# A two-block transformer layer kernel on one core: sums folded in the last up block, output rows added in memory by DMA, a reordered second norm, and queries and keys projected from consecutive tokens

## The reference, cut to what matters

```python
x = x + _rmsnorm_2(mix, g_mix_post[l])
h2 = _rmsnorm_2(x, g_mlp_pre[l])
ff = jnp.einsum('bsf,fd->bsd',
                jnp.square(jax.nn.relu(jnp.einsum('bsd,df->bsf', h2, w_up[l]))), w_down[l])
x = x + _rmsnorm_2(ff, g_mlp_post[l])
```

```python
q = _partial_rope(q.reshape(b, s, N_ATT_HEADS, HEAD_DIM), positions)
k = _partial_rope(k.reshape(b, s, N_ATT_HEADS, HEAD_DIM), positions)
```

## Time and profile before

| what | us |
|---|---|
| median of 3 runs | 2628.11 |
| lowest and highest run | 2627.49 and 2632.41 |
| the profiled execution | 2632.22 |
| span of the core in it | 2630.4 |
| PE busy in the span | 2522.1 (96%) |
| DVE, ACT, POOL busy | 1557.1, 852.1, 688.8 |

### The profile page before, as it was taken

How to read it: one execution, slowest core, us unless ns; L and a number is a source line. 1 busy time by engine, 2 the same in 40 slices (tenths; PEclk the granted TensorE clock), 3 DMA queues, 4 the chain that set the end, 5 groups by cost and what they waited for, 6 DMA issues and landing times. The chain is left out here.

```text
span 2630.4 us, 31418 instructions
## 1 busy us (share of the span) xinstructions
PE 2522.1 (96%) x12016; PEld 2105.4 (80%) x12016; DVE 1557.1 (59%) x2472; ACT 852.1 (32%) x1664; POOL 688.8 (26%) x656
## 2 busy tenths in 40 slices
PE   7999999999999999989999999999989999999995
PEld 4787889987899887778888888878867788887874
DVE  5611348888778686564655612124466857768588
ACT  4212231122311132462023133330145545354452
POOL 3422223333234232322533422224210000000002
PEclk8999999999999999999999999999999999999998
DMA  7311222213231222633443122225249574766753
GB/s 249 100 49 44 67 65 60 67 43 97 81 90 49 70 95 78 217 105 124 128 144 122 41 88 65 72 78 185 90 153 274 134 201 120 195 185 165 192 120 112
DMA packets 163514, 303.45 MB, mean 115 GB/s; under 512 B 22178, under 2 KB 46498, under 8 KB 159524
## 3 DMA queue, kind: packets, MB, share of 16 engines
q1 hardware_dynamic: 144164, 255.30, 29.6%
q0 software_dynamic: 18048, 41.95, 9.0%
q10 hardware_dynamic: 1152, 4.19, 0.4%
HBM read 235.12 MB, written 57.87 MB: 111 GB/s over the span
## 5 line engine op out<-in xcount | busy, mean ns | idle before, releaser
L2236 PE MATMUL ps<-act_hi,w_hi 128*128 128x512 f32 x1344 | 541.0, 403 | 14.4 <-DVE act_lo L1503 4.1
L1053 POOL CAST w_hi<-raw 128x512 fp32r<-128x512 f32 x288 | 216.0, 750 | 1248.6 <-DMA raw<-in_w_in 797.6
L2236 PE MATMUL ps<-act_lo,w_hi 128*128 128x512 f32 x1344 | 535.9, 399 | 0.0
L2236 PE MATMUL ps<-act_hi,w_lo 128*128 128x512 f32 x1344 | 528.2, 393 | 0.0
L1624 DVE SCALAR_TENSOR_TENSOR scr<-scr,small 128x512 f32<-128x512 f32 x480 | 430.4, 897 | 15.6
L1055 POOL TENSOR_TENSOR w_lo<-raw,w_hi 128x512 fp32r<-128x512 f32 x288 | 403.9, 1403 | 23.1
L2236 PE MATMUL ps<-w_hi,act_hi 128*128 128x512 f32 (+1 forms) x960 | 384.6, 401 | 2.8 <-POOL w_lo L1055 2.1
L2236 PE MATMUL ps<-w_lo,act_hi 128*128 128x512 f32 (+1 forms) x960 | 373.7, 389 | 0.0
L2236 PE MATMUL ps<-w_hi,act_lo 128*128 128x512 f32 (+1 forms) x960 | 373.5, 389 | 0.0
L2463 PE MATMUL ps<-w_hi 128*128 128x512 f32 x896 | 350.8, 391 | 21.0 <-DVE w_lo L2015 11.3
L2463 PE MATMUL ps<-w_hi,w_lo 128*128 128x512 f32 x896 | 349.2, 390 | 0.0
(11 more groups left out here) (222 smaller groups left out, 2706.1 us busy)
## 6 DMA issues: line engine op xcount, KB each, us to landing
raw<-in_w_in SPq DMA_DIRECT2D x176, 256.0 KB, 3.3
late_hi<-h2c_d SPq DMA_DIRECT2D x21, 1024.0 KB, 8.0
vreg<-in_w_ada SPq DMA_DIRECT2D x48, 256.0 KB, 4.0
raw<-in_w_in SPq DMA_DIRECT2D x72, 128.0 KB, 2.4
x_d<-big SPq DMA_DIRECT2D x16, 512.0 KB, 4.0
late_lo<-in_w_up SPq DMA_DIRECT2D x8, 1024.0 KB, 6.5
late_lo<-in_w_up POOLq DMA_DIRECT2D x8, 1024.0 KB, 12.8
raw<-in_w_up POOLq DMA_DIRECT2D x8, 1024.0 KB, 11.4
```

Source lines behind the costliest of these rows:

```text
L1053: pool.tensor_copy(dhi, src).then_inc(w_hi_done, 1)
L2236: ins = nc.tensor.matmul(out_, lhs, rhs, start=(m == 0), stop=(m == 3 * nk - 1))
```

## The change

- **Queries and keys.** `token_block(g, B)` becomes `token_block(g if name == "v" else 0, B)`: q and k are projected from consecutive tokens in every group; v as before. ACT's copy of a turned q or k tile of groups 1 and 2 now sorts the tokens: it reads PSUM with a step of 4 or 8 elements and writes runs of 32 or 16 elements. `rotate` takes the table row of the consecutive block.
- **The second norm.** ACT's first root of B comes before `turned_copy(B - 2)`; `weight_hi(0)` moves from B = 4 to B = 2; `act_hi_of(0)` is halved over B = 5 and 6, and a half of `act_hi_of(1)` comes at B = 7. DVE makes the halves of `act_lo_of(0)` right after the `evac_out` of B = 6 and B = 7, and halves of `act_lo_of(1)` around `norm_two(7)`. SP loads the first weight quarter one block earlier.
- **POOL's order of weight adds.** In each block the add into slot 0 (`t1_sum`) is issued before that into slot 1 (`t3_sum`).
- **Sums.** In the last up block (6), at its products 0 to 4, `fold_quarter` joins the running sums of blocks 1 to 5 by five instructions of 128x2048; in block 7, `mid` is overwritten in place of added to, product 5 is added into both `sum5` and `sum3`, and three folds per tile are gone.
- **The end.** The second norm stores its rows to the output itself (`x2_d` is gone), and after `final_scale(B)` POOL issues a DMA that adds the block onto those rows in device memory. `final_scale` is spread through the last product.

```diff
-                        if B == 2:
+                        if B == 1:
                             sp.wait_ge(w_ready, NP0)
                             weight_load(0, 0)
...
-                sp.dma_start(x2_d[P * B:P * B + P, :], tokT[:, B, :]).then_inc(n_st[1], 16)
+                sp.dma_start(out[P * B:P * B + P, :], tokT[:, B, :]).then_inc(n_st[1], 16)
...
-            for B in range(NB):
-                if B >= 2:
-                    sp.wait_ge(n_y[2], B - 1)
-                sp.dma_start(res2[B % 2], x2_d[P * B:P * B + P, :]).then_inc(n_ld[2][B % 2], 16)
-                if B >= 2:
-                    sp.dma_start(out[P * (B - 2):P * (B - 1), :], tokT[:, B - 2, :]).then_inc(out_st, 16)
...
             for blk in range(BLOCKS):
+                pool.wait_ge(wc_lo, 2 * at_product(blk, 1) + 2)
+                weight_add(0, weight_quarter(blk, 0, 1), t1_sum)
                 pool.wait_ge(wq_ld[1], 16 * (blk + 1))
                 weight_add(1, weight_quarter(blk, 1, 1), t3_sum)
-                pool.wait_ge(wc_lo, 2 * at_product(blk, 1) + 2)
-                weight_add(0, weight_quarter(blk, 0, 1), t1_sum)
...
+            pool.wait_ge(n_st[1], 16 * NB)
             for B in range(NB):
                 pool.wait_ge(n_scaled, B + 1)
-                pool.wait_ge(n_ld[2][B % 2], 16 * (B // 2 + 1))
-                pool.tensor_tensor(tokT[:, B, :], tokT[:, B, :], res2[B % 2], ALU.add).then_inc(n_y[2], 1)
+                pool.dma_start(out[P * B:P * B + P, :], tokT[:, B, :], accum_op=ALU.add).then_inc(out_st, 16)
+            pool.wait_ge(out_st, 16 * NB)
...
+                    if g in (1, 2):
+                        dst = (qT if name == "qt" else kT)[:, :, :]
...
+                            dst = dst.rearrange("p k (r j) -> p k r j", r=8)[:, :, :, 16 * B:16 * B + 16]
+                            src = src.rearrange("p (k j r) -> p k r j", k=4, r=8)
+                        nc.scalar.activation(dst, src, ACT.Copy).then_inc(free_of(u), 1)
...
                 for B in range(NB):
                     if B >= 2 and r == 0:
                         turned_hi(name, B - 2)
-                    elif B >= 2:
-                        turned_copy(B - 2)
-                    if r and B == 4:
-                        weight_hi(0)
-                    if r and B == 6:
-                        act_hi_of(0)
...
                     mean_square_root(r, B, 0, n_s1[r])
+                    if B >= 2 and r:
+                        turned_copy(B - 2)
+                        if B == 2:
+                            weight_hi(0)
+                        elif B >= 5:
+                            act_hi_of((0, 0, 1)[B - 5], ((0,), (1,), (0,))[B - 5])
                     norm_second(r, B)
...
                     evac_out(r, B, 1, NB + B)
+                    if r and B >= 6:
+                        act_lo_of(0, (B - 6,))
                     if B >= 1:
                         norm_two(r, B - 1)
...
                     norm_one(r, B)
-                    if r and B == NB - 1:
-                        act_lo_of(0)
+                if r:
+                    act_lo_of(1, (0,))
                 norm_two(r, NB - 1)
...
-                    add(mid, before(6))
+                    if end:
+                        dve.wait_ge(folded, 5)
+                    add(mid, -1 if end else before(6))
...
                     add(sum5, before(5))
+                    if end:
+                        add(sum3, before(3))
                 elif p == 3:
-                    add(sum3, before(3))
-                    if end:
-                        wait_used(dve, n, t)
-                        fold(sum3, sum5, ALU.add)
+                    add(sum3, at_product(blk, 5) if end else before(3))
...
-                        fold(sum7, mid, ALU.add)
...
+            FOLDS = ((sum7, mid, ALU.add, (7, 6)), (sum3, sum5, ALU.add, (3, 5)), (sum3, mid, ALU.subtract, ()),
+                     (sum5, sum7, ALU.subtract, ()), (sum4, sum7, ALU.add, (4,)))
...
+                nc.vector.tensor_tensor(dst, dst, a, op).then_inc(folded, 1)
...
+                if blk == BLOCKS - 2 and q < 5:
+                    fold_quarter(q)
+                if n == PRODUCTS - 1:
+                    final_scale(0)
                 evict(n, 0)
+                if n == PRODUCTS - 1:
+                    final_scale(1)
                 evict(n, 1)
...
+                if n == PRODUCTS - 1:
+                    final_scale(2)
                 evict(n, 2)
                 if n == PRODUCTS - 2:
                     dve.wait_ge(bc_ld, 96)
-                    for B in range(4):
+                elif n == PRODUCTS - 1:
+                    for B in (3, 4, 5):
                         final_scale(B)
-                elif n == PRODUCTS - 1:
-                    final_scale(4)
-                    final_scale(5)
                     evict(n, 3)
                     final_scale(6)
                     final_scale(7)
...
-                    blk = token_block(g, B)
+                    blk = token_block(g if name == "v" else 0, B)
```

More of the change, by code:

```diff
@@ L322, in build @@
         s1_buf = quarter(hi_flat, 2)
-        res2, junk2 = [hi_flat[:, 2048 + i * S:2048 + (i + 1) * S] for i in range(2)], hi_flat[:, S:2 * S]
+        junk2 = hi_flat[:, S:2 * S]
         wq = [raw[:, :, :], quarter(lo_flat, 1), quarter(lo_flat, 0), quarter(scr, 0)]
@@ L526, in at_product, with uses @@
             return 7 * blk + ORDER.index(p)
-        USES = ({p: 1 for p in ORDER}, {p: 2 if p == 1 else 1 for p in ORDER})
+        def uses(blk, p):
+            return 2 if blk % 2 and p == 1 or blk == BLOCKS - 1 and p == 5 else 1
         used_before, total = [], [0, 0]
@@ L947, in _ @@
                         if B >= 2:
[L948 to L949 removed]
+                            sp.dma_start(out[P * (B - 2):P * (B - 1), :], tokT[:, B - 2, :]).then_inc(n_st[1], 16)
+                        if B == 1:
                             sp.wait_ge(w_ready, NP0)
@@ L1007, in _ @@
             sp.dma_start(bc[2][0], A["g_mlp_post_2"][0].partition_broadcast(P)).then_inc(bc_ld, 16)
[L1008 to L1017 removed]
+            sp.wait_ge(n_st[1], 16 * NB)
             sp.wait_ge(out_st, 16 * NB)
@@ L1405, in weight_hi, with act_hi_of @@
                     nc.scalar.activation(hi[:, two, :], src[:, two, :], ACT.Copy).then_inc(wc_hi, 1)
-            def act_hi_of(n):
+            def act_hi_of(n, halves=(0, 1)):
                 blk, p = product(n)
@@ L1422, in act_hi_of @@
                 wait_set(act, n)
-                for j in range(2):
+                for j in halves:
                     nc.scalar.activation(hi[:, 2 * j:2 * j + 2, :], src[:, 2 * j:2 * j + 2, :], ACT.Copy
@@ L1468, in act_step_of @@
                         copy_used(n, t, (h21 if p == 1 else h22)[:, t, :])
+            act_hi_of(1, (1,))
             turned_copy(6)
-            act_hi_of(1)
             weight_hi(1)
@@ L2007, in weight_lo_of, with act_lo_of @@
                                             ).then_inc(wc_lo, 1)
-            def act_lo_of(n):
+            def act_lo_of(n, halves=(0, 1)):
                 src, (hi, lo) = act_quarter(n), act_split(n)
-                for j in range(2):
+                for j in halves:
                     two = slice(2 * j, 2 * j + 2)
@@ L2094, in evict_down @@
                                                 ).then_inc(row_done, 1)
-                        fold(sum7, mid, ALU.add)
                 elif p == 7:
                     if end:
-                        settle()
-                    add(sum7, before(7))
-                    if end:
+                        dve.wait_ge(row_done, t + 1)
+                        add(mid, at_product(blk, 6))
                         wait_used(dve, n, t)
-                        fold(sum5, sum7, ALU.subtract)
-                        fold(sum4, sum7, ALU.add)
+                        fold(sum5, mid, ALU.subtract)
+                        fold(sum4, mid, ALU.add)
+                    else:
+                        add(sum7, before(7))
                 else:
@@ L2107, in evict_down, with fold_quarter @@
                     add(sum4, before(4))
+            FOLDS = ((sum7, mid, ALU.add, (7, 6)), (sum3, sum5, ALU.add, (3, 5)), (sum3, mid, ALU.subtract, ()),
+                     (sum5, sum7, ALU.subtract, ()), (sum4, sum7, ALU.add, (4,)))
+            def fold_quarter(i):
+                dst, a, op, last = FOLDS[i]
+                for p in last:
+                    for t in range(4):
+                        wait_used(dve, at_product(BLOCKS - 3, p), t)
+                if i:
+                    dve.wait_ge(folded, i)
+                nc.vector.tensor_tensor(dst, dst, a, op).then_inc(folded, 1)
             def evict(n, t):
@@ L2158, in _ @@
                     act_sums(blk, (4,))
-                if n + 1 < PRODUCTS:
+                if n == 0:
+                    act_lo_of(1, (1,))
+                    weight_lo_of(1)
+                elif n + 1 < PRODUCTS:
                     weight_lo_of(n + 1)
```

19 lines of the change are left out of this document (13 added, 6 removed).

## The result

| what | before, us | after, us |
|---|---|---|
| median (4 runs each, side by side) | 2627.8 | 2595.45 |
| lowest and highest run | 2625.8 and 2632.4 | 2594.3 and 2596.7 |
| the profiled execution | 2632.22 | 2596.56 |
| span of the core in it | 2630.4 | 2594.4 |

The ratio after to before is 0.9872 (95% interval 0.9859 to 0.9885). The kernel is 32.4 us faster by the medians and 36.0 by the two spans; the prediction had 38.1 and 38.2, a median of 2590 and a range of 2580 to 2602. So the forecast's own mechanism decided, and 5.4 us of it were missing.

A forecast was written before the change was run, and what follows sets the result against it. PE's matmuls at pace were taken to bound the kernel, busy for 2522.1 of 2630.4 us. The terms -9.9 - 18.2 - 10.1 = -38.2, taken from the median 2628.1, gave 2590, range 2580 to 2602.

The forecast's parts named there:

- Part 1: Queries and keys of groups 1 and 2: consecutive tokens shorten units, -2.3 and -7.6, together -9.9 us; at best 12.9.
- walked: Hand walk of sixteen q and k units with DVE's rotation times: group 1 104.4 us, group 2 102.1 with shorter units.
- The price of the step itself: Stationary operand's step in q and k units: 0.29 us per unit in group 1, 0.52 in group 2.
- Part 2: Second norm: new order of ACT and DVE lets PE start product 1 at 1970.7 rather than 1989.05, -18.2 us.
- up to 2 us: Before product 3: DVE's sums wait for stores of h2 in a busy DMA queue, so this much may come back.
- Part 3: Last up block: five fold instructions, 11.5 us of DVE, lie in its idle time, so PE doesn't see them.
- Part 4: Tail after the last matmul: earlier scales and eight accumulating DMAs at 2.6 us each end the span at 2620.3, -10.1 us.
- the norm's wait is only replaced: Rival, before product 3: DVE's sums wait for the filled queue, PE loses 8 of the 18.2 us: 2598; 12%.
- The accumulating DMAs are slower: Rival, the end: with their target in device memory, at 3.9 us each, the tail keeps its 30.25: 2600; 17%.
- The step isn't the cause: Rival, q and k units: the step doesn't lengthen them, so part 1 does nothing: 2600; group 1 alone 2592; 4%.
- Slower than before: Rival, the end: the eight DMAs don't overlap, each waiting out its own latency; at 9 us each 2641; 3%.
- more is won: Rival: DVE's bursts don't bind (-3.0) and the DMAs pass faster (-4): 2583; 15%.

The follow-up runs named there:

- steps: Changed kernel with fewer group 1 taps, q and k stationary operands at steps 2, 4, 8 and 1: 6.04, 6.20, 6.44 and 5.92 us a unit.
- plain_end: Changed kernel with POOL's eight output DMAs as plain stores, residual left out of the output: 2585.4 us, 0.9838 of the kernel before.
- only_end: Kernel before with only the folds, the spread scales and the accumulating output DMAs: 2620.2 us, 0.9967 of the kernel before.
- only_norm: Kernel before with only the reordered second norm, SP's earlier weight load and POOL's order of weight adds: 2611.3 us, 0.9934 of the kernel before.

## Why the prediction was right, and where it was off

- **Part 1, -9.9.** Group 2 came as walked: -7.8 for -7.6. Group 1 was walked at -2.3 and gave 0.3 in this pair of traces and 1.3 over ten. The step that failed is the price of a wait for a rotation. I gave it none beyond its length, where the slower clock behind it can add 1.6 us (eight matmuls at 0.43 instead of 0.23); in the traces without that spell group 1 wins 2.0. DVE's time in a burst, taken over unchanged from the old timeline, is the smaller part: one burst took 7.2 us rather than 6.2, a length that the trace of before already had elsewhere, and the stretch took 105.2 at a full clock for a walked 104.4. The price of the step itself (0.29 and 0.52) stands, as steps shows, and ACT's sorting copy costs nothing beyond the plain one, as assumed.
- **Part 2, -18.2.** 18.2 by the stretches; product 1 was to start 45.2 us after the turn of block 0 and started 45.3 after it. The loss of "up to 2 us" before product 3 came to 1.9. I named it and left it out of the sum; the hand walk had left this low part a slack of 0.3 us, too little to count as none, and the loss belonged in the sum. Its chain was also longer than I had it: not the stores alone but ACT's squares ahead of the high part.
- **Part 3, at nothing.** No wait of PE appears in the last up block, and product 3 to the last matmul takes as long as before (587.6 and 587.7 us). The folds are hidden.
- **Part 4, -10.1.** 8.6 was measured. The pace of 2.6 us a block was 2.7, a lone DMA 5.6 us was 5.3, the last scale came 7.3 us after the last matmul for 8.0, and the last landing 19.7 after it, where 19.75 was forecast. The sum of that landing had a slip: 2595.7 + 3.0 + 8 x 2.6 is 2619.5 and not 2619.9, so by its own terms it was due 19.35 after the last matmul. (The "one alone" with 8.6 us was the first DMA of the same pair, too; the pace was rightly read from the pair, and 3.0 stands where the text has 3.5 around.) What failed is the small term behind: I took 0.4 us from the last landing to the end, and it is 2.0 with POOL's queue (in plain_end as well).
- **The median.** The two spans differ by 36.0, close to the 38.2, but 3.2 of that is the start, by which the profiled execution of before was late. Taking the parts from the median was right; by this pair of traces the 5.4 us between 2590 and 2595.45 are group 1 (2), the wait before product 3 (1.9) and the end (1.5). The first of these is in good part a slow spell that other traces don't have.
- **Rivals.** Of "the norm's wait is only replaced" a quarter came (1.9 of 8). "The accumulating DMAs are slower" fell: reading and writing device memory they keep the pace that one into SBUF had. "The step isn't the cause" fell, for group 1 as well. "Slower than before" fell too: a lone DMA takes 5.3 us and eight land 2.7 apart, so they overlap. (Its limit of 7.4 us is 2.6 + 38.2 / 8; the terms printed for it, 30.25 - 4.4 + 28.1 over eight, give 6.7.) Of "more is won" nothing came.

What stays open: why the clock falls behind some of PE's pauses and not behind others. In the kernel before, a wait of 2.0 us in group 1 left it at 1.00; in only_end the same stretch has 0.98 and takes 108.34 us. The length of the pause alone does not decide it either. Behind the 3.3 us before product 3 the kernel after keeps a full clock, and behind 3.2 us in the same place only_norm does not:

```profile
1985.18:1990.50 5.32, 5.32 (x24) 4.40 (x24) 1.03 (x1) 3.10 (x6) 0.00 (x0) 1.00 1.10 261
```

```profile
1990.10:1995.40 5.30, 5.26 (x16) 4.21 (x17) 1.08 (x1) 2.99 (x6) 0.00 (x0) 0.68 1.10 262
```

Such slow spells of about 1.6 us are in some traces and not in others whose program is the same up to there. Whether they make most of the spread between executions no run shows, since only one execution of each kernel was traced.

## What to carry to other kernels

An engine that is off the critical path but near its limit decides what a faster bottleneck is worth: before costing such an edit, look at how long the other engine's longest burst is against the new, shorter unit. When work is put off, ask what waits for its completion and which transfers stand behind that wait in the same queue; here eight late taps cost over 12 us, some 4 of them through a queue of loads and some 4 through the softmax behind them. An accumulating DMA takes an add and a load away, but it has a pace of its own, so its blocks should start as soon as their data is final and be spread over the work that remains.

## What the runs showed of the hardware

- A stationary operand read with a step makes a unit of 24 matmuls and four turns dearer at every doubling: 5.92, 6.04, 6.20 and 6.44 us for steps of 1, 2, 4 and 8 float32 elements. The units without a wait or a slow clock in that trace all agree with these to 0.05 us. ACT's read of PSUM at steps of 4 and 8 costs nothing: 594 ns for 128x512, as the plain copy.
- An accumulating DMA of 512 KB onto device memory lands after 5.1 to 5.3 us alone, and a train of them at 2.5 to 2.7 us each, with one gap of 3.7. The same blocks as plain stores land after 3.0 us.
- A wait of PE of 3.3 us in group 1 was followed by eight matmuls of 128x512 at half clock, 1.6 us more on top of it; a wait of the same length before product 3, in the same execution, was not.
- From the landing of the last DMA to the end of the span it took 2.0 us with POOL's queue and 0.4 us with SP's.
